# Layer norms by token, the router on raw x, and a new buffer order for the first nine expert chunks

## What is computed

```python
h = _layer_norm(ALPHA * h + m[2] * mixer(_modulate(h, m[0], m[1])), ln_g[i, 0], ln_b[i, 0])
h = _layer_norm(ALPHA * h + m[5] * _hier_moe(_modulate(h, m[3], m[4])), ln_g[i, 1], ln_b[i, 1])
```

## Time and profile before

| | us |
|---|---|
| median of 3 runs | 2212.3 (2211.49 to 2212.36) |
| the profiled execution | 2211.73 |
| its span in the trace | 2209.9 |
| TensorE busy | 2117.2 |
| VectorE busy | 940.2 |
| ScalarE busy | 566.5 |

### The profile page before, as it was taken

How to read it: one execution, slowest core, us unless ns; L and a number is a source line. 1 busy time by engine, 2 the same in 40 slices (tenths; PEclk the granted TensorE clock), 3 DMA queues, 4 the chain that set the end, 5 groups by cost and what they waited for, 6 DMA issues and landing times.

```text
span 2209.9 us, 31040 instructions
## 1 busy us (share of the span) xinstructions
PE 2117.2 (96%) x12934; PEld 1470.8 (67%) x12934; DVE 940.2 (43%) x1857; ACT 566.5 (26%) x1058; POOL 0.8 (0%) x6
## 2 busy tenths in 40 slices
PE   8999999999999999999988999999988999999987
PEld 7876779998877889998977544443335644443333
DVE  6898735542643345566365511211113512111112
ACT  2124123331135033344245311111112311111112
POOL 0000000000000000000000000000000000000000
PEclk9999999999999999999998999999999999999999
DMA  6445664546435654534240999999999699999995
GB/s 273 152 153 229 256 239 153 190 183 261 166 115 216 252 214 178 189 120 159 77 190 13 427 424 426 426 426 428 424 427 427 245 423 425 426 426 428 427 425 211
DMA packets 50079, 621.23 MB, mean 281 GB/s; under 512 B 5552, under 2 KB 5680, under 8 KB 12080
## 3 DMA queue, kind: packets, MB, share of 16 engines
q1 hardware_dynamic: 49824, 619.53, 68.8%
q10 hardware_dynamic: 144, 0.13, 0.0%
HBM read 618.59 MB, written 1.05 MB: 280 GB/s over the span
## 4 chain that ended last, share of the span: by engine, by line
PE 75%; DMA 15%; DVE 7%; ACT 1%; issue 1%; SPq 0%; ACTq 0%; DVEq 0%
PE bank L651 21%; DMA ring<-in_experts 12%; PE bank L1332 12%; PE bank L1355 7%; DMA arena<-in_experts 3%; PE sums L871 3%; PE sums L870 3%; PE sums L869 3%; PE bank L869 3%; PE bank L870 3%; PE bank L871 3%; PE sums L1365 2%; PE bank L1018 2%; PE bank L1020 2%; PE bank L1019 2%; DVE wide L2009 2%
## 5 line engine op out<-in xcount | busy, mean ns | idle before, releaser
L651 PE MATMUL bank<-h,ring 128*128 128x256 f32 x1568 | 345.7, 381 | 0.0
L651 PEld LDWEIGHTS bank<-h,ring 128*128 128x128 f32 x1568 | 297.1, 191 | 47.9 <-issue 6.5
L2241 DVE TENSOR_TENSOR ring_split<-ring,arena_split 128x2048 fp32r<-128x2048 f32 x64 | 144.2, 2289 | 150.7 <-ACT arena_split L1633 150.5
L2690 DVE TENSOR_TENSOR wide<-bank,wide 128x256 f32<-128x256 f32 x64 | 27.2, 425 | 385.3 <-ACT wide L1831 385.3
L2697 DVE SCALAR_TENSOR_TENSOR scratch_split<-bank,small,wide_split 128x512 fp32r<-128x512 f32 x64 | 48.1, 751 | 272.4 <-ACT wide_split L1839 272.4
L1633 ACT ACTIVATE arena_split<-ring 128x2048 fp32r<-128x2048 f32 x64 | 119.3, 1906 | 157.8 <-PE sums L871 144.1
L1332 PE MATMUL bank<-ring,h 128*64 128x512 f32 x640 | 143.7, 595 | 15.1 <-DMA ring<-in_experts 15.1
L1332 PE MATMUL bank<-arena,wide 128*64 128x512 f32 x608 | 137.0, 595 | 10.9 <-DMA arena<-in_experts 10.8
L869 PE MATMUL bank<-h_split,arena_split 128*128 128x256 f32 x512 | 145.8, 285 | 1.5 <-DVE scratch_split L2263 1.5
L869 PE MATMUL sums<-smax_split,arena_split 128*128 128x256 f32 x512 | 144.9, 283 | 0.0
L870 PE MATMUL sums<-smax_split,arena_split 128*128 128x256 f32 x512 | 144.9, 283 | 0.0
(11 more groups left out here) (387 smaller groups left out, 3600.1 us busy)
## 6 DMA issues: line engine op xcount, KB each, us to landing
ring<-in_stream SPq DMA_DIRECT2D x99, 2048.0 KB, 7.7
ring<-in_experts SPq DMA_DIRECT2D x96, 2048.0 KB, 29.4
arena<-in_experts SPq DMA_DIRECT2D x72, 2048.0 KB, 27.2
arena<-in_experts SPq DMA_DIRECT2D x22, 1024.0 KB, 23.9
stat<-in_experts SPq DMA_DIRECT2D x22, 512.0 KB, 24.8
scratch<-in_experts SPq DMA_DIRECT2D x22, 512.0 KB, 26.8
extra<-in_experts SPq DMA_DIRECT2D x2, 2048.0 KB, 26.8
arena<-in_stream SPq DMA_DIRECT2D x1, 2048.0 KB, 29.3
```

The source lines that it names most:

```text
L651: mm = pe.matmul(dst, a, b, start=(first and i == 0), stop=(i == len(terms) - 1))
L2241: dve.tensor_tensor(split["ring"][:, slot, 2048 * part:2048 * part + 2048], v, HI[("up", "down")[part]][:, j % 2, :].bitcast(F32), ALU.sub ...
```

## The change

It has two parts. First, the statistics of the four norms are taken by token. TensorE transposes raw `x` into rows by token and, in the same pass, multiplies it with a column of 1/1024 (s = 0, beside the 36 router columns) or with ones (s = 1) for the means. VectorE centres the rows, ScalarE squares them with an accumulated sum, and root and reciprocal are over two columns. The centred rows go back to features by a product with a diagonal of the reciprocal roots (`rows_back`), and from its banks `h` and the scaled `x` are made with gain and shift. The router is applied to raw `x`: gain and shift of the norm are folded into its weights and bias before (`sum_router`, a product with ones, `fold_router`), and its mean part is subtracted from the weights. The gathered tokens get gain and shift when they are kept. Filler counts change: 9 and 5 in place of 3, 10 and 7, and the pool's 4 goes.

Second, the nine first chunks are assigned to slots by a table, and sent in that order.

```diff
-    ("b_router", 2 * 36), ("w_router", 2 * KT * 36)])
+    ("b_router", 2 * 36), ("w_router", 2 * KT * 37)])
...
+        FIRST_SLOTS = (0, 1, 8, 6, 2, 3, 4, 5, 7)
+
         def expert_slot(q, first):
 
             if first and q <= EXPERT_RING:
-                return q
+                return FIRST_SLOTS[q]
             return (q - 1) % EXPERT_RING
...
                     sp.wait_ge(S.sem("moe0_down_done"), rounds_more[0] * EXPERTS + (EXPERTS - 3))
-                    load_expert_chunk(sp, S, i, 0, EXPERT_RING, first=True)
-                    for q in range(1, EXPERT_RING - 1):
-                        used(0, rounds_more[0] * TURN_PAIRS, EXPERTS * EXPERT_CHUNKS - EXPERT_RING + 1 + q)
-                        load_expert_chunk(sp, S, i, 0, q, first=True)
+                    load_expert_chunk(sp, S, i, 0, FIRST_SLOTS.index(EXPERT_RING), first=True)
+                    for slot in range(1, EXPERT_RING - 1):
+                        used(0, rounds_more[0] * TURN_PAIRS, EXPERTS * EXPERT_CHUNKS - EXPERT_RING + 1 + slot)
+                        load_expert_chunk(sp, S, i, 0, FIRST_SLOTS.index(slot), first=True)
                     S.wait(sp, "chunk_used", C_POOL)
                     load_expert_chunk(sp, S, i, 0, 0, first=True)
+                    S.wait(sp, "filled", "pool_rows", 0)
+                    load_expert_chunk(sp, S, i, 0, EXPERT_RING, first=True)
+
+                def freed_by_mixer(q):
+
+                    slot = FIRST_SLOTS[q]
+                    if slot == 0:
+                        S.wait(sp, "filled", "ret", 1)
+                    elif slot == 1:
+                        sp.wait_ge(S.sem("ret_ready"), S.value("ret_ready", 0))
+                    elif slot == EXPERT_RING:
+                        S.wait(sp, "read", "s", "na", 15)
+                    elif slot == EXPERT_RING - 2:
+                        S.wait(sp, "filled", "y", "na", 3)
+                    elif slot == 2:
+                        S.wait(sp, "chunk_used", C_POOL - 1)
+                    elif slot == EXPERT_RING - 1:
+                        S.wait(sp, "filled", "router_fold")
...
-                        if first and EXPERT_RING < q <= 2 * EXPERT_RING:
-                            used(i, done, q - EXPERT_RING - 1)
-                        elif not start or q > EXPERT_RING:
+                        slot = expert_slot(q, first)
...
+                        elif first and q <= 2 * EXPERT_RING:
+                            used(i, done, FIRST_SLOTS.index(slot))
+                        else:
                             used(i, done, q - EXPERT_RING)
...
             out_half(0, 1, 1)
+            S.wait(pe, "router_summed", 0)
+            bank = open_bank(pe, "router_fold")
+            filled(pe.matmul(bank[:, 0:144], ones, fold_out, start=True, stop=True), "router_fold")
             out_half(1, 1, 0)
...
+                def features(pairs):
+
+                    for k in range(2 * pairs[0], 2 * pairs[-1] + 2):
+                        for t in range(2):
+                            rhs = w[:, k, :] if s == 0 else cst("ones", 0, 2)
+                            mm = pe.matmul(means[t][:, 0:(2 if s else 37)], x[:, k, t * P:(t + 1) * P], rhs,
+                                           start=(k == 0), stop=(k == KT - 1))
...
                 for b in range(4):
                     pe.wait_ge(S.sem("added"), S.value("added", i, s, b))
+                    for t in range(2):
+                        at = token_bank(s, t, b // 2)
+                        S.note(("bank", "xt", i, s, t, b // 2), "bank", at)
+                        for k in (2 * b, 2 * b + 1):
+                            mm = transposed((banks + sums)[at][:, k % 4 * P:(k % 4 + 1) * P], x[:, k, t * P:(t + 1) * P])
...
+            def rows_back(i, s):
+
+                pe.wait_ge(S.sem(f"diag{s}"), S.value(f"diag{s}", i))
...
+                        for t in range(2):
+                            at = k % 2 * T + t * P
+                            mm = pe.matmul(bank[:, at:at + P], centred_rows(s, t, k * P, P), diag_rstd[:, t, :],
+                                           start=True, stop=True, skip_group_check=True)
...
+                rows_back(i, 0)
+                keep_clock(5)
 
                 S.wait(pe, "members", i)
...
+                        S.wait(pe, "read", "back", i, 0, j)
                         gather(0, j, banks[first_banks[j]])
...
-            keep_clock(4)
             pool_band_of(2)
...
+                act.activation(small[:, 130:131], eps_ln, ACT.Sqrt)
+                for half in range(2):
+                    for t in range(2):
+                        S.wait(act, "centred", i, s, t, half)
+                        ins = act.activation(M["by_token"][:, t, 512 * half:512 * half + 512], centred_rows(s, t, 512 * half, 512),
+                                             ACT.Square, accum_out=square_sums[:, t, half:half + 1])
+                S.give(ins, "squared", i, s)
...
+            norm_columns()
+            sum_router()
+            ab_low(C_ABOUT + 1, 1, 0)
             scale_x()
-            norm_columns()
+            fold_router()
...
             residual(0, 0, 2, ab_bank, None)
+            clear_for_route()
             post_norm(0, 0)
...
-                    ins = dve.tensor_tensor(lg[:, t, :], bank[:, t * 64:t * 64 + 36], prm("b_router", 36 * i, 36), ALU.add)
+                    bank = bank_of("means", i, 0, t)
+                    ins = dve.scalar_tensor_tensor(out=lg[:, t, :], in0=bank[:, 0:36], scalar=token_rstd[:, t:t + 1],
+                                                   in1=prm("b_router", 36 * i, 36), op0=ALU.mult, op1=ALU.add)
...
-                    dve.tensor_copy(flat2(gathered[buf][:, 2 * j:2 * j + 2, :]), bank[:, :])\
-                       .then_inc(S.sem(f"moe{i}_gather_kept"), 1)
+                    for q in range(2):
+                        k = 2 * j + q
+                        ins = dve.tensor_scalar(gathered[buf][:, k, :], bank[:, q * T:(q + 1) * T], norm_col(i, 0, "h_gain", k),
+                                                norm_col(i, 0, "h_shift", k), ALU.mult, ALU.add)
+                    ins.then_inc(S.sem(f"moe{i}_gather_kept"), 1)
```

More of the change, by code:

```diff
@@ L1291, in moe @@
                 zero_sums("read", "rank", i)
-                first_banks = [b for half in range(2) for b in sorted(S.of("bank", "rows", i, t, half)[1] for t in range(2))]
+                first_banks = [S.of("bank", "back", i, 0, b)[1] for b in range(4)]
                 def raised(kind, it, add, per_turn):
@@ new lines, in post_norm @@
+                for half in range(2):
+                    for t in range(2):
+                        S.wait(act, "centred", i, s, t, half)
+                        ins = act.activation(M["by_token"][:, t, 512 * half:512 * half + 512], centred_rows(s, t, 512 * half, 512),
+                                             ACT.Square, accum_out=square_sums[:, t, half:half + 1])
+                S.give(ins, "squared", i, s)
+                S.wait(act, "token_var", i, s)
+                S.give(act.activation(token_root, token_var, ACT.Sqrt, scale=1.0 / D, bias=eps_ln), "token_root", i, s)
@@ new lines, in post_norm @@
+                if s == 0:
+                    S.wait(act, "token_rstd", i, s)
+                    for t in range(2):
+                        ins = act.activation(diag_rstd[:, t, :], ident, ACT.Copy, scale=token_rstd[:, t:t + 1])
+                    S.give(ins, "diag0", i)
+                    return
+                for b in (0, 2):
+                    bank = take(act, "back", i, s, b)
+                    for q in range(2):
+                        k = 2 * b + q
+                        if i:
+                            ins = act.activation(x[:, k, :], bank[:, q * T:(q + 1) * T], ACT.Identity, scale=prm("ln_g", 3 * KT + k),
@@ L1869, in post_norm @@
                                                  bias=prm("ln_b", 3 * KT + k))
                         else:
[L1871 to L1885 removed]
+                            ins = act.activation(h[:, k, :], bank[:, q * T:(q + 1) * T], ACT.Identity,
+                                                 scale=norm_col(i, s, "h_gain", k), bias=norm_col(i, s, "h_shift", k))
@@ new lines, in post_norm, with scale_x @@
+                    S.give(ins, "h_ready_by_act", i, s, b)
+                if i == 0:
+                    scale_x(i, s)
+            def scale_x(i, s):
+                for b in range(4):
+                    bank = take(act, "back", i, s, b)
+                    if s and b % 2:
+                        S.wait(act, "h_ready_by_dve", i, s, b)
+                    for q in range(2):
+                        k = 2 * b + q
+                        ins = act.activation(x[:, k, :], bank[:, q * T:(q + 1) * T], ACT.Identity, scale=norm_col(i, s, "x_gain", k),
+                                             bias=norm_col(i, s, "x_shift", k))
+                    read("x_scaled", S.give(ins, "x_scaled", i, s, b), "back", i, s, b)
```

(19 more changed lines are left out.)

250 lines of the change are left out of this document (112 added, 138 removed).

## The result

Twenty runs of each kernel on one chip: 2216.3 us (2214.39 to 2219.47) after, 2212.32 us (2208.54 to 2213.95) before; ratio 1.0021, 95% interval 1.0015 to 1.0027. The change makes the kernel slower by 4.0 us. The interval leaves out a ratio of 1, but the size is at the edge of the 0.2% (4.4 us) that the prediction took as what can be told from no change: 2216.3 is 0.4 under its line of 2216.7. 2217.3 was predicted. The profiled execution took 2214.61 us, with a span of 2212.8.

A forecast was written before the change was run, and what follows sets the result against it. The expert stages were taken as bound by their DMA streams. Layer 0's end +0.7 (+6.05 - 5.35), interlude -3.7, layer 1's stream +7.35 and last norm +0.7 total +5.05 on 2212.3: 2217.3 us, own range 2215.5 to 2221.

The forecast's parts named there:

- The ring term: Both expert stages: new slots make chunks 11 and 12 wait longer; streams 6.05 and 7.35 us later for the same G.
- G: Start of the first expert's gate product in a layer; predicted at 1236.4 in layer 0 and 1741.2 in layer 1.
- Rival A: Expert streams: the ring's order costs nothing and the DMA never runs dry; 2201.8 us, chance 0.08.
- The early loads: Layer 0: chunks 2 and 3 sent in idle DMA time, worth 2 x 4.9 us of stream, counted inside the 6.05.
- G earlier by 5.6 a norm: Norms before the experts: first sum or transpose to G takes 24.2 us where it took 29.8.
- Rival B: All norms shorten by 0.3 to 2 us more than counted, paying for most of the ring; 2214 us, chance 0.30.
- The rule on short passes: TensorE in the norms: float32 passes of 128 columns or fewer advance by 0.112 to 0.13 us; 0.116 was used.
- Rival B2: TensorE in the norms: short passes 0.081 us apart, faster than any row; 2206 us, chance 0.03.
- The interlude: From the end of layer 0's experts to layer 1's G: +1.6 and -5.3, so 3.7 us shorter.
- norm (0,1): Norm after layer 0's experts, ahead of the pool stage: 14.9 us where it took 13.3, 1.6 longer.
- Rival C: TensorE's clock falls in the norms, through gaps between filler and other products: +6 us, 2223.5 us, chance 0.10.
- Last norm: Norm at the kernel's end, behind layer 1's experts: 0.7 us longer, with nothing to hide it.

The follow-up runs named there:

- e3: Kernel before with only the new slot table and order of sending, norms as before: 2225.55 us, ratio 1.0065.
- e1: Kernel after with the old slot table and old order of the first nine loads, so the new norms and router alone: 2209.88 us, ratio 0.9994.
- e2: As e1, old slots, but in layer 0 the nine chunks are sent as their slots come free, chunks 8 and 6 early: 2203.69 us, ratio 0.9973.
- e4: Kernel after with the ring walked in another slot order from chunk 9, so later chunks wait for the one eight ahead: 2211.3 us, ratio 1.0.
- e5: Kernel after, but in layer 0 chunks 2 and 3 go out only behind the mixer's last use of its weights: 2217.7 us, ratio 1.0024.
- e10: Kernel after with the edits of e2, e6 and e9 together: 2199.9 us, ratio 0.9943.
- e9: Kernel after with the pool's four filler products put back, in the wait itself, ahead of the third band product's bank: 2215.23 us, ratio 1.002.
- e6: Kernel after with 64 columns of ones in place of 2 in the mean products of the norms behind the experts: 2212.06 us, ratio 0.9998.
- e11: e10 with two fillers in place of five behind the rows that go back, in the norms before the experts: 2198.5 us.

## Why the prediction held, and where its terms were off

**The ring term (+6.05 and +7.35): right in mechanism and in sum.** Measured +7.3 and +6.3 (442.8 to 450.1, 443.7 to 449.9), 13.5 against 13.4; that the sum is so close is luck, since layer 0 was sized 1.2 too low and layer 1 1.1 too high. The sends at G + 20.33 and G + 26.66 are the predicted waits for chunks 4 and 5. e3 shows the term without the norms, e1 and e2 show it gone with the old slots, and e4 shows it shrink when the distance is shortened. Chunk 12 landed at G + 34.5 in layer 0 (sent at 1259.51, 7.8 us), as predicted. What was off lies behind it. The prediction held that both streams of before "never pause" behind chunk 12; in layer 1 of before only 368 GB/s moved from 1784.15 to 1789.15 (423 at the same distance from G in the kernel after), worth some 0.7 us at 426. In layer 0 after, chunk 14 landed at G + 44.8, 0.6 later than two chunks of 4.9 us behind chunk 12; the rest is open. Rival A needed chunk 4 to be used by G + 13.5; it was used at G + 20.3.

**The early loads: right in kind.** The prediction counted them inside the +6.05, and held that the pause for chunk 12 would stand in the stream's way whatever went out early. e5 puts them at 1.3 us under the new slots. What it didn't say, and e2 showed, is that they are worth 6.0 us under the old ones: the order of sends was good, and its slots spoiled it.

**G earlier by 5.6 a norm: a little low in layer 0.** From the first transpose to G, 23.5 us against 29.8, so 6.3. The 48 passes took 5.1 us and not 5.6: from the first transpose (1209.32) to the filler behind them (1214.42), 0.106 a pass. The last read of the squares was over 9.0 us in (9.7), the logits began at 9.7 (10.5). The rank products began 1.4 us late behind the filler (1.75). The rest of the earlier G, 2.6 of 8.9 us, isn't the change's: the mixer ended earlier in that execution (see the last section). Rival B, that the norms would pay for most of the ring, got 0.7 us in this one.

**The rule on short passes.** The shortest spacing in the new norms is 0.10 us (eight products of 37 columns, 0.81 us from the first of them at 1213.61 to the filler at 1214.42); the 32 of the rows that go back are 0.115 apart (3.67 us to the filler at 1223.48). Rival B2 is out. The Trainium skill's 81 ns, page TensorE: Matmul & The Clock Gate, section Back-to-back issue gap, isn't reached in float32 in these products; here the measurement decides.

**The interlude (-3.7): the step that failed, -1.6 measured.** By the starts on TensorE's timelines (1687.99, 1701.25, 1714.52 and 1744.15 before; 1686.36, 1702.79, 1716.85 and 1740.91 after) it splits into norm (0,1), from 13.3 to 16.4 (+3.2, predicted +1.6); the pool stage, 13.3 to 14.1 (+0.8, predicted nothing); norm (1,0), 29.6 to 24.1 (-5.6, predicted -5.3). Rival C, the falling clock in all norms, was given 0.10 and a price of 6 us; it came in the norms behind the experts and in the pool, and the 2.1 us by which the interlude missed are a third of that. With the clock held, the terms are those predicted or better: norm (0,1) 14.4 us in e10 (1682.25 to 1696.68; predicted 14.9), the interlude 54.3. "The pool stage's filler lay in a wait: nothing" was the error of kind: it lay in a wait, and what it did there was to keep the clock up for the 2 us of products behind it and the next norm's start. e9 puts that at 1.7 us.

**Last norm (+0.7): -0.1 measured**, and 21.6 against 22.1 with the clock held. The new norm is a little shorter there too, although its 18 fillers took 5.76 us in the kernel after, at a fallen clock. The four squares took 2.7 us (2201.02 to 2203.72) of the 3.0 counted; where the rest of the 0.8 lies wasn't looked for.

In sum, -2.63 for the mixer, then -6.28, +7.27, -1.60, +6.27 and -0.13 make +2.90, the difference of the two spans; the medians differ by 4.0. Without the mixer it is +5.53, against 5.05 predicted. That closeness is partly offset: the interlude was sized 2.1 too low and layer 0's stream 1.2, while the first norm, layer 1's stream and the last norm were sized 0.9, 1.1 and 0.8 too high. The errors of the single terms are 6.1 us without their signs and 0.5 with them, so the total owes a good part of its closeness to luck.

**The prediction's own signs of being wrong.** It named three. Chunk 12 earlier than G + 26: no, it went at G + 26.66. G at 1233 or before: yes, 1232.85, but only with the 2.6 us of the mixer's earlier end; the norm alone would have made it 1235.5. The clock below 1.00 in a norm: yes, 0.57 from 1690 to 1698, without any such luck in it. So by its own test the part on the norms' clock was wrong, and its claim that the clock "stays at 1.00 through the present gaps of a norm" didn't carry over to the new norms. Of its three outcomes it gave slower, above 2216.7, 0.55; the median, 2216.3, is just inside what it called the same, at 0.34.

## What to carry to other kernels

Where a load goes decides what the loads behind it wait for. A place outside the ring must hold the chunk that is needed last of the first set: given to an early one, it shortens the ring's distance for all that follow. Send order and placement are two choices; here one was worth 6 us and the other cost 13. And where TensorE waits or makes very narrow products just ahead of a critical stretch, look at the granted clock of that stretch before taking filler out; put filler ahead of the semaphore that really ends last, or it becomes work.

## What the runs showed of the hardware

**Narrow products let the clock fall though the engine is never idle.** In the kernel after, TensorE waits for 0.57 us until the norm's first transpose at 1686.36, and so it does in e6 (1686.11). From 1686.4 to 1689.0 it is busy for 2.47 of 2.60 us in both, and then without a gap. The window just ahead of the fall, in the kernel after:

```profile
1689.00:1691.10 2.10, 2.10 (x22) 2.10 (x22) 0.00 (x0) 0.00 (x0) 0.00 (x0) 1.00 0.97 414
```

From 1691.10 to 1692.50 it is busy for all 1.40 us at 0.53. In e6 both windows are as busy (2.10 of 2.10, 1.40 of 1.40) and both at 1.00. Over the longer window of the kernel after, it is busy for all 8.00 us from 1690 to 1698 at a granted clock of 0.57; with 64 columns in the products ahead, it is busy for 6.93 of 8 at 1.00. The width cost nothing: 1.00 us for eight products of 64 columns, 0.95 for eight of 2. So a busy share near 10 tenths doesn't tell that the clock is safe; only its own column does.

**The fall has no fixed length.** At the same place the 18 fillers took 5.64 (e1), 6.80 (after), 7.17 (e5) us against 4.13. In e5 the half clock lasted into the next norm and cost 5 us of interlude. That this is what spreads the times isn't shown: the kernel after spreads over 5.1 us in its 20 runs and e6 over 3.5 in 11, but the kernel before, whose profile has 1.00 in the norms, spreads over 5.4 in 20.

**Two starts.** SyncE's first send behind the mixer comes at 1208.90 to 1209.72 in seven profiles and at 1211.61 to 1212.24 in six, in kernels of every kind. The difference is there long before the changed part, in the first block. The first operation of VectorE from `bank` and `wide` behind 185 us (128x128) starts at 188.41 to 189.30 in the seven and at 191.25 to 191.91 in the six. A part of it comes before 20 us: VectorE's first reciprocal starts at 15.26 to 16.08 in the seven and at 16.47 to 17.12 in the six. And from 175 to 180 the granted clock is 1.00 in all seven and 0.74 to 0.83 in all six. That window in before (late) and in the kernel after (early):

```profile
175.00:180.00 5.00, 3.23 (x21) 1.97 (x20) 1.74 (x8) 3.18 (x10) 0.00 (x0) 0.83 0.98 413
175.00:180.00 5.00, 3.56 (x21) 2.95 (x22) 2.53 (x9) 2.79 (x11) 0.00 (x0) 1.00 1.03 439
```

The clock just ahead of the send doesn't tell the two apart: from 1140 to 1150 it is 0.84 to 0.88 in the six, but 0.83 in two of the seven (e4, e11) and 1.00 in the others. Why an execution is early or late at 17 us, and why the clock falls at 175, is open. Spans should be compared from that send on, as the table does.
